# The last branch's eight gates move from beside the delta rule to beside the differential attention, and ScalarE instead of GpSimd scales the delta rule's keys and values

## What is computed

```python
xn = rmsnorm(x, norm1_g[l])
h = xn @ w_in[l]                       # 5920 columns, split among four mixers
y_a = gdn_mixer(a_qkv, a_z, a_ab, ...) # gated delta rule, 4 heads, both directions
y_b = diff_mixer(b_q, b_k, b_v, ...)   # differential attention, 4 heads
y_c = swa_mixer(c_q, c_k, c_v, ...)    # sliding-window attention, 8 heads
y_d = mlstm_mixer(d_q, d_k, d_v, ...)  # mLSTM, 4 heads, both directions
branch = einsum('bsnw,nwd->bsnd', [y_a, y_b, y_c, y_d], w_branch[l])
gate = sigmoid(einsum('bsd,dne->bsne', xn, w_gate[l]))
x = x + sum(gate * branch, axis=2) @ w_out[l]
xn = rmsnorm(x, norm2_g[l])
x = x + square(relu(xn @ w_mlp1[l])) @ w_mlp2[l]
```

## Time and profile before

| | us |
|---|---|
| median of 3 runs (4109.19 to 4118.03) | 4112.58 |
| the profiled execution | 4104.98 |
| its span | 4103.1 |
| TensorE busy in the span | 3538.1 (86%) |
| VectorE | 2207.3 (54%) |
| ScalarE | 1426.7 (35%) |
| GpSimd | 557.5 (14%) |

### The profile page before, as it was taken

The page is one execution under the profiler, slowest core; times in us unless marked ns, Lnnn a source line. Parts: engine busy times, 40 slices in busy tenths (PEclk is TensorE's granted clock), DMA queues, the critical chain, the costliest instruction groups (busy, mean ns, idle before and its releaser), DMA issues. The chain is left out here.

```text
span 4103.1 us, 48477 instructions
## 1 busy us (share of the span) xinstructions
PE 3538.1 (86%) x17676; PEld 2902.6 (71%) x17676; DVE 2207.3 (54%) x4200; ACT 1426.7 (35%) x2664; POOL 557.5 (14%) x436
## 2 busy tenths in 40 slices
PE   7887888878789999778879999889998779789997
PEld 5666667666577888556767888668887557577886
DVE  3566634656427875566654333237775656663333
ACT  3313333133324443334434332334442334444321
POOL 1000010000003333111011110003333100112110
PEclk9988889888899999899989999989999889899999
DMA  4620036311253222222223333342222212433332
GB/s 128 180 86 27 20 93 175 91 37 32 50 149 109 73 74 60 70 57 81 79 71 108 98 95 95 101 135 83 78 73 85 59 51 59 109 88 93 95 95 72
DMA packets 554066, 350.07 MB, mean 85 GB/s; under 512 B 73412, under 2 KB 497348, under 8 KB 553564
## 3 DMA queue, kind: packets, MB, share of 16 engines
q1 hardware_dynamic: 553820, 346.84, 29.8%
HBM read 301.36 MB, written 45.42 MB: 85 GB/s over the span
## 5 line engine op out<-in xcount | busy, mean ns | idle before, releaser
L556 PE MATMUL bank<-h,w_hi 128*128 128x512 f32 x2240 | 960.2, 429 | 161.1 <-DVE w_low L549 119.7
L557 PE MATMUL bank<-h,w_hi 128*128 128x512 f32 x2240 | 908.0, 405 | 0.0
L558 PE MATMUL bank<-h,w_low 128*128 128x512 f32 x2240 | 906.4, 405 | 0.0
L543 ACT CAST w_hi<-w 128x1024 fp32r<-128x1024 f32 (+2 forms) x456 | 434.0, 953 | 656.1 <-DMA w<-in_w_mlp 393.6
L549 DVE TENSOR_TENSOR w_low<-w,w_hi 128x1024 fp32r<-128x1024 f32 (+2 forms) x456 | 530.5, 1164 | 237.7 <-ACT w_hi L543 231.4
L556 PEld LDWEIGHTS bank<-h,w_hi 128*128 128x128 f32 x2240 | 439.8, 196 | 282.0 <-DVE w_low L549 141.3
L558 PEld LDWEIGHTS bank<-h,w_low 128*128 128x128 f32 x2240 | 438.6, 196 | 101.9
L557 PEld LDWEIGHTS bank<-h,w_hi 128*128 128x128 f32 x2240 | 441.0, 197 | 91.2 <-issue 9.5
L557 PE MATMUL bank<-yT_low,w_hi 128*128 128x512 f32 x768 | 313.2, 408 | 0.0
L1173 ACT ACTIVATE prob<-bank,softmax_stat 128x512 f32<-128x512 f32 (+3 forms) x256 | 145.3, 569 | 288.2 <-DVE softmax_stat L1205 222.7
L556 PE MATMUL bank<-yT_low,w_hi 128*128 128x512 f32 x384 | 166.5, 434 | 56.0 <-DVE xT L685 42.4
(11 more groups left out here) (426 smaller groups left out, 6072.3 us busy)
## 6 DMA issues: line engine op xcount, KB each, us to landing
w<-in_w_in SPq DMA_DIRECT2D x148, 512.0 KB, 4.2
w<-in_w_mlp SPq DMA_DIRECT2D x128, 512.0 KB, 4.0
z<-z_tile SPq DMA_DIRECT2D x164, 256.0 KB, 4.3
w<-in_w_gate SPq DMA_DIRECT2D x64, 512.0 KB, 4.2
q_twice<-z SPq DMA_DIRECT2D x128, 128.0 KB, 2.9
w<-in_w_branch SPq DMA_DIRECT2D x64, 256.0 KB, 2.9
k_twice<-z SPq DMA_DIRECT2D x88, 128.0 KB, 3.6
w<-in_w_out SPq DMA_DIRECT2D x32, 256.0 KB, 2.9
```

The source lines that it names most:

```text
L543: self.a.copy(self.wh[s][:, 0:d, 0:n], self.w[s][:, 0:d, 0:n]).then_inc(self.w_high.sem, 1)
L556: self.t.matmul(bank[0:n, :], wh, high, start=j == 0, stop=False)
L557: self.t.matmul(bank[0:n, :], wh, low, start=False, stop=False)
L558: return self.t.matmul(bank[0:n, :], wl, high, start=False, stop=j == self.depth(i) - 1)
```

## The change

Four things. The limit beside `Gdn` is gate 3 instead of gate 0, so the eight gate units (32 pieces) come under `Diff`, which then has 80. The shares follow: 0.7 in the levels, 0.3 in the scan, one piece less before A and before the output's transposes; 1.4 in `Diff`. `head_act` scales keys and values, four 128x128 activations at a time behind the copies of X of each level, and `head_pool` keeps the masks and, in levels 5 and 6, the two products of q. The bookkeeping of row tiles no longer assumes that the units that go to memory are the first ones of the list; the order of the units is the same.

```diff
--- before.py
+++ after.py
@@ -497,7 +497,7 @@
         self.w_in = [self.sig(f"w_in{i}", -(-N // S), by=16) for i in range(S)]
         self.w_high, self.w_low = self.sig("w_high", N), self.sig("w_low", N)
         self.multiplied, self.drained = self.sig("multiplied", N), self.sig("drained", N)
-        self.row_out = [self.sig(f"row_out{i}", -(-self.kept // 3), by=16) for i in range(3)]
+        self.row_out = [self.sig(f"row_out{i}", -(-self.kept // 3) + 1, by=16) for i in range(3)]
         self.running = self.engines()
         self.halts, self.limit = 0, 0
 
@@ -744,7 +744,12 @@
         with_row = [(kind, s, e) for kind, s, e in self.units if kind in ("z", "gate") or (kind, s) == ("branch", 3)]
         self.row = {unit: r for r, unit in enumerate(with_row)}
         self.row.update({("branch", s, e): self.row["gate", s, e] for s in range(3) for e in range(KD)})
-        self.kept = self.z_tiles + KD
+        to_memory = [i for i, (kind, s, e) in enumerate(self.units) if kind == "z" or (kind, s) == ("gate", 3)]
+        self.kept, self.nth_out, self.outs = len(to_memory), {}, [0, 0, 0]
+        for i in to_memory:
+            slot = self.row[self.units[i]] % 3
+            self.nth_out[i] = self.outs[slot]
+            self.outs[slot] += 1
         self.init_woven(k.A["norm1_g_2"][l])
         by_act = [kind in ("z", "gate") for kind, _, _ in self.units]
         self.order = [by_act[:i].count(by_act[i]) for i in range(len(self.units))]
@@ -809,9 +814,9 @@
 
         if r < 3:
             return
-        kind, s, e = next(u for u, n in self.row.items() if n == r - 3 and (u[0] == "branch" or n < self.kept))
-        if r - 3 < self.kept:
-            eng.wait_ge(*self.row_out[r % 3]((r - 3) // 3))
+        kind, s, e = next(u for u, n in self.row.items() if n == r - 3 and (u[0] == "branch" or self.at[u] in self.nth_out))
+        if kind != "branch":
+            eng.wait_ge(*self.row_out[r % 3](self.nth_out[self.at[kind, s, e]]))
         elif s == 0:
             eng.wait_ge(*self.done(self.at[kind, s, e]))
         else:
@@ -822,17 +827,18 @@
             e = self.units[i][2]
             r = self.row[self.units[i]]
             if e == 0:
-                self.wait_stored(self.s, self.kept - 1)
+                for slot in range(3):
+                    self.s.wait_ge(*self.row_out[slot](self.outs[slot] - 1))
             self.wait_row_free(self.s, r)
             self.s.dma_start(self.rows[r % 3][:, :], self.k.z3[e * P:(e + 1) * P, :]).then_inc(self.gate_in[e % 3].sem, 16)
 
     def store(self, i):
-        if 0 <= i < self.kept:
+        if i in self.nth_out:
             kind, _, e = self.units[i]
-            n = self.width(i)
+            n, slot = self.width(i), self.row[self.units[i]] % 3
             self.s.wait_ge(*self.done(i))
             out = (self.k.z2 if kind == "z" else self.k.z3)[e * P:e * P + n, :]
-            self.s.dma_start(out, self.rows[i % 3][0:n, :]).then_inc(self.row_out[i % 3].sem, 16)
+            self.s.dma_start(out, self.rows[slot][0:n, :]).then_inc(self.row_out[slot].sem, 16)
 
     def sp(self):
         self.gained_sp()
@@ -2406,7 +2412,7 @@
 
 
 
-    H, share = 4, 0.85
+    H, share, scan_share = 4, 0.7, 0.3
 
     def __init__(self, k, l, stream):
         super().__init__(k)
@@ -2611,7 +2617,7 @@
             m = t_.matmul(bank[1][:, ch[t]], kT[:, ch[t]], qT[:, ch[t]], start=True, stop=True)
         m.then_inc(self.kq_made.sem, 1)
         yield 3.0
-        yield 3.0
+        yield 2.0
         for d in range(2):
             t_.wait_ge(*self.A_made(h, d))
             for t in range(NT):
@@ -2667,7 +2673,7 @@
                     if n == 1:
                         t_.wait_ge(*self.q_decayed(h, d))
                     t_.matmul(bank[3 + 2 * d][:, 0:P], self.qdec[d][:, ch[t]], self.state[d][:, :], start=True, stop=False)
-            yield self.share
+            yield self.scan_share
             for d in range(2):
                 t = NT - 1 - n if d else n
                 if n == 0:
@@ -2680,8 +2686,8 @@
                 if n < NT - 1:
                     t_.matmul(bank[2 + 2 * d][:, P:2 * P], buf["kdec"][d][:, t, :], V, start=True, stop=True).then_inc(self.kV_made.sem, 1)
                 t_.matmul(bank[3 + 2 * d][:, 0:P], buf["aT"][d][:, t, :], V, start=n == 0, stop=True).then_inc(self.o_summed.sem, 1)
-            yield self.share
-        yield 2.0
+            yield self.scan_share
+        yield 1.0
         t_.wait_ge(*self.o_normed(h))
         for t in range(NT):
             m = t_.transpose(bank[5][:, ch[t]], self.osum[:, t, :], ident)
@@ -2714,6 +2720,15 @@
                 a.wait_ge(*self.LM_made(h, s - 1, d))
                 a.copy(flat(buf["X"][d]), bank[2 + 2 * d][:, :]).then_inc(self.X_made.sem, 1)
             yield
+            d, n = divmod(s - 1, 3)
+            if s == 1:
+                a.wait_ge(*self.hq_made(h))
+                a.wait_ge(*self.tok_made(h, 1))
+            name, src, i = (("vb", self.vtok, 0), ("kbe", self.ktok, 1), ("kdec", self.ktok, 3))[n]
+            for t in range(NT):
+                m = a.activation(buf[name][d][:, t, :], src[:, t, :], ACT.Copy, scale=self.hq[:, i, t, d:d + 1])
+            if name == "kdec":
+                m.then_inc(self.kv_scaled.sem, 1)
             yield
         for d in range(2):
             a.wait_ge(*self.U_summed(h, d))
@@ -2848,24 +2863,17 @@
             p.wait_ge(*self.AT_made(h, d))
             p.tensor_tensor(buf["LT"][d], buf["AT"][d], self.level("levlow" if d else "levup", 1), ALU.mult).then_inc(self.L_made.sem, 1)
         yield
-        p.wait_ge(*self.tok_made(h, 1))
-        later = [(d, name) for d in range(2) for name in ("vb", "kbe", "kdec", "q")]
         for s in range(1, LEVELS):
             if s > 1:
                 for d in range(2):
                     p.wait_ge(*self.LM_made(h, s - 2, d))
                     p.tensor_tensor(buf["LT"][d], buf["AT"][d], self.level("levlow" if d else "levup", s), ALU.mult).then_inc(self.L_made.sem, 1)
             yield
-            for d, name in later[2 * s - 2:2 * s]:
-                if name == "q":
-                    p.wait_ge(*self.q_moved(h))
-                    p.wait_ge(*self.q_exp(h, d))
-                    p.tensor_tensor(self.qdec[d][:, :], self.qdec[d][:, :], self.q_now[:, :], ALU.mult).then_inc(self.q_decayed.sem, 1)
-                else:
-                    src, i = {"vb": (self.vtok, 0), "kbe": (self.ktok, 1), "kdec": (self.ktok, 3)}[name]
-                    m = p.tensor_tensor(buf[name][d], src[:, :, :], self.hq[:, i, :, d:d + 1].to_broadcast(self.W4), ALU.mult)
-                    if name == "kdec":
-                        m.then_inc(self.kv_scaled.sem, 1)
+            if s > LEVELS - 3:
+                d = s - (LEVELS - 2)
+                p.wait_ge(*self.q_moved(h))
+                p.wait_ge(*self.q_exp(h, d))
+                p.tensor_tensor(self.qdec[d][:, :], self.qdec[d][:, :], self.q_now[:, :], ALU.mult).then_inc(self.q_decayed.sem, 1)
             yield
         for _ in range(1 + 2 * NT + 2):
             yield
@@ -2963,7 +2971,7 @@
 
 class Diff(Attention, Rotation, NormedHeads):
     maps, mixes = 2, True
-    score_banks, other_banks, share = 2, ((2, 3), (4, 5)), 0.85
+    score_banks, other_banks, share = 2, ((2, 3), (4, 5)), 1.4
 
     def __init__(self, k, l, stream):
         super().__init__(k)
@@ -3466,9 +3474,8 @@
 def layer_two(k, l):
     stream = Through(k, l)
     stream.go_to(("z", 0, (C2["a_ab"] + 15) // P + 2))
-    stream.until(("gate", 0, 0))
-    Gdn(k, l, stream).beside(stream)
-    stream.go_to(("gate", 3, 0))
+    stream.until(("gate", 3, 0))
+    Gdn(k, l, stream).beside(stream, ("gate", 3, 0))
     stream.branches()
     stream.until(("gate", 1, 0))
     Diff(k, l, stream).beside(stream, ("gate", 1, 0))
```

## The result

The changed kernel takes 4119.94 us (median of 20 runs, 4112.93 to 4132.63), the one before 4112.31 us (20 runs): a ratio of 1.0021, 95% interval 1.0012 to 1.0031. It is slower by 8 us, where 12 us faster had been forecast. The profiled execution took 4118.53 us, with a span of 4116.7.

The account below looks back on a forecast made before the run. TensorE, busy for 86% of the span, was taken as the bound. Delta rule -34 us and attention with sliding-window stage +28.2 left -5.8 a layer, -12 in all: 4100 us, range 4076 to 4124.

Parts of the forecast that it names:

- (10): Attention, second rotation: half of the added fill is hidden by VectorE's work beside GpSimd's, -3.5 us (0 to -7).
- (2): Delta rule levels: TensorE still sets the period; without GpSimd's scalings 4 us of waits are saved (0 to 9).
- (6): Delta rule: waits of 4 to 6 us are followed by a stretch at 1.2 GHz, +3 us (0 to +7).
- (5): Delta rule, normed output of a head: less fill before the wait, waits rise from 12.7 to 20.4 us, +7.7.
- (8): Attention steps: fill behind the values can't shorten the 2.16 us wait for mixed probabilities; 13.2 pieces are paid in full.
- (9): Attention, first rotation: the 6 pieces added there cost nothing, first scores come when they did before, -8.3 us.
- (11): Attention: the waits for normed heads, 10.0 us, get shorter, -3.0 us.
- (12): Attention: splitting the first branch's input moves from the stage's start, where it was hidden, into the steps, +2 us.
- (13): Attention's end: 5.6 pieces over its last copies, -0.8 us; the sliding-window stage starts at full clock sooner, -2.
- A: Rival: denser attention raises its clock to 0.93 and saves 12 us there, 4080 us in all; chance 0.17.
- B: Rival: the rotations' fill is not hidden as weights arrive late, +12 us a layer, 4124 us; chance 0.16.
- C: Rival, no change: ScalarE's chain bounds the delta rule's shortened scan, 6 us a layer lost, 4112 us; chance 0.22.

Follow-up runs that it names:

- level_to_norm: Changed kernel with 2.8 pieces a head taken from the delta rule's levels, 2.6 more put ahead of the wait for its normed output: 4078.35 us.
- rot_less: Changed kernel with half the fill (0.7 instead of 1.4) in the ten places of the attention's second rotation, seven pieces coming later: 4122.83 us.
- scan_to_norm: Changed kernel with the 2.4 pieces a head of the delta rule's scan put ahead of the wait for its normed output: 4113.75 us.
- norm_fill: Changed kernel with 5 instead of 2 pieces ahead of each of the attention's two waits for normed heads: 4119.57 us.
- level_to_tail: Changed kernel with 2.8 pieces a head taken from the delta rule's levels and done at its end with nothing beside them: 4129.10 us.

## Why the prediction was wrong

The step that failed is the attention's sum, and in it (10), the second rotation: it had 3.5 us of the added fill hidden there by VectorE's work, and the stretch took 3.3 us more than its fill. That is 6.8 of the 7.3 us by which the attention is longer than forecast. In all the sum let 13.6 us of the attention's idle time a layer be filled (-8.3, -3.5, -3.0, +2 and -0.8); it was 2.0. The delta rule missed by 3.3 us more, by (2) and (6). Per layer, from the first:

| | forecast | measured |
|---|---|---|
| delta rule, 32 pieces | -43.8 | 192 products fewer |
| its idle time | +6.9 | +6.8 (43.1 to 49.9) |
| its own time besides | +3 | +6.4 (busy -37.4) |
| **window** | **-34** | **-30.6** |
| attention, 32 pieces | +43.8 | 192 products more |
| its idle time | -13.6 | -2.0 (53.0 to 51.0) |
| its own time besides | 0 | -4.3 (busy +39.5) |
| sliding-window stage | -2 | -3.1 |
| **attention and sliding-window stage** | **+28.2** | **+34.4** |

The delta rule's idle time came out as forecast by luck: (2) gave 3.2 us less than forecast and (5) took 3.1 us less. The attention by stretches, with the pieces of the stream in each (counted from the products):

| first attention | pieces | us | longer by | the added pieces alone |
|---|---|---|---|---|
| up to the first mixed probabilities | 15, now 22 | 52.2, now 53.7 | 1.5 | 9.6 |
| steps of the first pair, to the normed heads | 10, now 16 | 52.3, now 60.5 | 8.2 | 8.2 |
| second rotation, to the first mixed probabilities | 13, now 20 | 39.2, now 52.1 | 12.9 | 9.6 |
| steps of the second pair, to the normed heads | 10, now 16 | 52.9, now 58.8 | 5.9 | 8.2 |
| behind the last wait | 0, now 6 | 3.7, now 12.7 | 9.0 | 8.2 |

- (1), (7): right, 32 pieces each way.
- (2): -4 was forecast, and it was -0.8, out of two things that I had not kept apart. Waits for low parts fell by 7.1, and those for M, MT and the masked L rose by 6.3, as thinner fill uncovered VectorE's chain. That the scaling would matter little was right beside the old fill (3.2 us) and wrong beside the new one (12.8). The Trainium skill (SBUF — State Buffer, "SBUF: two separate sides") has a GpSimd instruction that reads SBUF and a VectorE instruction with two SBUF inputs exclude each other, where ScalarE never waits on either; VectorE's busy time agrees in both pairs of kernels, down by 12.8 and 14.9 us.
- (3): hidden, as forecast. The scaled activation of 128x128 is a median of 0.39 us instead of the 0.30 taken, within the bounds. The formula of the Trainium skill (ScalarE: Activation LUTs, "What ACT_TABLE_LOAD costs") gives an estimate of 386 ns with its pointer operand, and the trace agrees.
- (4), (5): the waits for the normed output became 17.3, not 20.4. Their size was nearly right and their meaning missed: I priced the pieces taken away from there as one more small cost, where level_to_norm shows that a piece put there cost nothing (10.4 pieces, 14.2 us, against 14.7 us less of waits), so that taking it away gives nothing back.
- (6): mis-sized. The delta rule's TensorE time besides the pieces grew by 6.4 instead of 3; the group of four transposes behind each of those waits takes 1.12, 1.12, 0.80 and 1.11 us, where it took 0.66, 1.11, 0.77 and 0.72. The 1.5 us before A did not come: that wait is 3.4 us in both kernels.
- (8): right. The 2.16 us waits stayed, and 12 more pieces in the steps (16.4 us) made them 14.1 us longer, at a higher clock (0.86 and 0.87 before, 0.94 and 0.93 now). It was also where the answer lay: the step said that fill behind the values can't shorten that wait, and did not ask what fill ahead of it would do.
- (9): right. Up to the first mixed probabilities 7 more pieces (9.6 us) made 53.7 us out of 52.2, 8 us hidden against 8.3.
- (10): wrong. Seven more pieces, 9.6 us, made the second rotation 12.9 us longer (39.2 to 52.1) instead of 6. With 13 pieces in it VectorE's and TensorE's work were about level; with 20 TensorE is the longer (busy for 44.7 us there, VectorE for 34.1), and rot_less shows that 7.5 to 8.8 of the 9.6 us are paid. Waits for low parts of 2.48 and 2.80 replace 1.69 and 2.11. The order of the program then puts three pieces between the last rotation and the v transposes, with nothing left to hide: VectorE was idle for 6.9 us. The 4 to 5 us that rot_less leaves over the kernel before are not explained.
- (11): wrong on the waits, though not on the window. The waits for normed heads are 10.7, not 7.0: before either wait the same 2.0 pieces are due as before, and the larger share of the steps had been used up in the steps (4.31 and 5.70 us became 5.33 and 5.34).
- (12), (13): the stage now ends in 12.7 us behind its last wait instead of 3.7, with six pieces (8.2 us) there. They are paid in full, as the 43.8 of (7) had them; the 0.8 taken off did not come, and no loss of 2 us shows in the steps. Taken together the steps and the end cost 1.5 us less than their pieces, where (11) to (13) had 1.8: right by luck, with higher waits and a higher clock against each other.

Of the rivals, A had its premise and not its consequence: the attention's clock rose from 0.86 to 0.92, its window to 237.7 instead of under 222, because the clock gave back 4.3 us, not 12. B's sign came true without its cause: the first scores come 44.2 us after the stage's start (43.0 before), not 50. C named the chain of ScalarE that scan_to_norm then showed, but as a loss beside the forecast, not as idle time that the change laid open.

Of the signs, the delta rule's windows (421.8 and 421.6 us), its longest wait for a normed output (4.7), its level periods (9.2, 7.5, 8.4 and 6.8 us from 1389.96 on) and the first scores agree; the attention's windows (237.7) lie outside their 226 to 236.

Not settled is the share of the clock. It moves with the waits (0.95 to 0.97 in level_to_norm) and no run changed it alone.

## What to carry to other kernels

Look for a stage's idle time at the places where its engine waits: ask of every moved piece what it stands in front of, and of every removed one what it had covered. Fill ahead of a wait is free only if its own inputs are ready: in norm_fill the waits for normed heads fell by 8.7 us, others rose, and the kernel's time stayed. Before moving work between stages, move it within them: 2.6 pieces a head set ahead of a wait, and 1.0 piece a step set between scores and transposes, were worth 42 and 37 us against the changed kernel, and after that the move between stages made no difference that the times can show (3 us a layer by the windows). A relief measured with ample fill (3.2 us for the scaling) says little about the same relief with thin fill (12.8).

## What the hardware showed unexpectedly

GpSimd's scalings stretched VectorE's work by 13 to 15 us a layer whether or not anything waited for it. And TensorE's own time for the same 2323 products was 371.9 or 365.3 us, by whether its waits for normed outputs (up to 4.7 us each) were covered; level_to_tail, where they were not, has 373.4.
